# Twelve norm statistics of a decoder trunk from rounded high and low parts of the squares, a fourth relevance buffer, and selection steps placed later

## The reference

```python
def rms_norm(x, gain):
    xf = x.astype(jnp.float32)
    y = xf * lax.rsqrt(jnp.mean(xf * xf, axis=-1, keepdims=True) + RMS_EPS)
    return (y * gain.astype(jnp.float32)).astype(x.dtype)
...
    q_d = rms_norm(heads(d_q, DSA_HEADS), dsa_q_norm)
    k_d = rms_norm(heads(d_k, DSA_HEADS), dsa_k_norm)
...
    q_m = heads(rms_norm(m_cq, mla_q_latent_norm) @ mla_w_uq, MLA_HEADS)
    kv_m = heads(rms_norm(m_ckv, mla_kv_latent_norm) @ mla_w_ukv, MLA_HEADS)
    q_m = rms_norm(q_m, mla_q_norm)
    k_m = rms_norm(jnp.concatenate([k_nope, k_rope], axis=-1), mla_k_norm)
...
        rel = jax.nn.relu(jnp.einsum('bqhd,bsd->bqhs', iqb, ik))
        score = jnp.einsum('bqhs,bqh->bqs', rel, iwb).astype(jnp.float32)
        score = jnp.where(visible[None], score, NEG_INF)
        _, idx = lax.top_k(score, top_k)
```

## Time and profile before

| what | value |
|---|---|
| median of 3 runs | 1255.1 us (1255.06 to 1255.46) |
| the profiled execution | 1255.26 us, of which its span is 1253.5 us |
| PE busy | 1237.1 us, 99% of the span |
| DVE busy | 751.8 us, 60% |
| ACT busy | 528.8 us, 42% |
| POOL busy | 217.1 us, 17% |
| granted TensorE clock | 1.00 of full speed throughout |
| chain that ended last | PE 92%, ACT 3%, DVE 3%, issue 1%, DMA 1% |

### The profile page before, as it was taken

How to read it: one execution, slowest core, us unless ns; L and a number is a source line. 1 busy time by engine, 2 the same in 40 slices (tenths; PEclk the granted TensorE clock), 3 DMA queues, 4 the chain that set the end, 5 groups by cost and what they waited for, 6 DMA issues and landing times.

```text
span 1253.5 us, 17688 instructions
## 1 busy us (share of the span) xinstructions
PE 1237.1 (99%) x5956; PEld 973.9 (78%) x5956; DVE 751.8 (60%) x1233; ACT 528.8 (42%) x858; POOL 217.1 (17%) x141
## 2 busy tenths in 40 slices
PE   9999999999999999999999999999999999999998
PEld 7766876688888888888886668767888888888887
DVE  6689868644644554544756898685446445445444
ACT  5674438644223224224436643586432242232331
POOL 1122330020120110200621334200201102102002
PEclk9999999999999999999999999999999999999999
DMA  6212220033233223323222212201232223233223
GB/s 245 86 51 67 68 85 2 18 101 123 92 101 100 98 86 100 100 88 99 98 85 85 67 51 85 68 2 40 95 100 87 99 100 101 84 100 100 96 94 111
DMA packets 30720, 108.36 MB, mean 86 GB/s; under 512 B 3536, under 2 KB 3536, under 8 KB 30672
## 3 DMA queue, kind: packets, MB, share of 16 engines
q1 hardware_dynamic: 29520, 103.82, 24.9%
q0 software_dynamic: 432, 2.86, 0.6%
q10 hardware_dynamic: 720, 1.07, 0.3%
HBM read 105.64 MB, written 2.10 MB: 86 GB/s over the span
## 4 chain that ended last, share of the span: by engine, by line
PE 92%; ACT 3%; DVE 3%; issue 1%; DMA 1%; ACTq 0%; DVEq 0%
PE bank L889 19%; PE bank L890 19%; PE bank L891 19%; PE bank L510 6%; PE bank L512 6%; PE bank L511 6%; PE bank L533 2%; PE bank L532 2%; PE bank L531 2%; PE bank L546 2%; PE bank L772 2%; PE bank L784 1%; PE bank L799 1%; PE bank L750 1%; DMA x<-in_x 1%
## 5 line engine op out<-in xcount | busy, mean ns | idle before, releaser
L944 ACT ACTIVATE wh<-raw 128x1024 fp32r<-128x1024 f32 x191 | 201.6, 1055 | 382.7 <-PE bank L891 246.5
L1267 DVE TENSOR_TENSOR wl<-raw,wh 128x1024 fp32r<-128x1024 f32 x155 | 241.2, 1556 | 75.8 <-ACT wh L944 75.7
L889 PE MATMUL bank<-hh,wl 128*128 128x512 f32 x512 | 200.0, 391 | 0.0
L889 PE MATMUL bank<-xmh,wl 128*128 128x512 f32 x512 | 199.3, 389 | 0.0
L891 PE MATMUL bank<-hl,wh 128*128 128x512 f32 x512 | 199.2, 389 | 0.0
L890 PE MATMUL bank<-xmh,wh 128*128 128x512 f32 x512 | 199.2, 389 | 0.0
L891 PE MATMUL bank<-xml,wh 128*128 128x512 f32 x512 | 199.2, 389 | 0.0
L890 PE MATMUL bank<-hh,wh 128*128 128x512 f32 x512 | 199.2, 389 | 0.0
L476 POOL TENSOR_TENSOR x<-x,rsb 128x512 f32<-128x512 f32 x63 | 83.3, 1322 | 589.3 <-DVE rsb L1688 589.3
L510 PE MATMUL bank<-xgh,wl 128*128 128x512 f32 x368 | 151.3, 411 | 3.6 <-DVE xgl L1280 3.4
L1677 DVE TENSOR_TENSOR sqb<-tf 128x512 f32<-128x512 f32 x64 | 44.3, 692 | 181.6 <-ACT hh L1230 181.6
(11 more groups left out here) (215 smaller groups left out, 1641.5 us busy)
## 6 DMA issues: line engine op xcount, KB each, us to landing
raw<-in_stream SPq DMA_DIRECT2D x191, 512.0 KB, 3.3
out_y<-x SPq DMA_DIRECT2D x8, 256.0 KB, 3.6
x<-in_x ACTq DMA_DIRECT2D x4, 256.0 KB, 6.9
x<-in_x SPq DMA_DIRECT2D x4, 256.0 KB, 7.2
con<-in_consts POOLq DMA_DIRECT2D x1, 976.5 KB, 5.2
par<-in_params POOLq DMA_DIRECT2D x1, 916.0 KB, 5.0
par<-in_params POOLq DMA_DIRECT2D x1, 896.0 KB, 6.9
raw<-in_stream SPq DMA_DIRECT2D x2, 256.0 KB, 4.2
```

The source lines that it names most:

```text
L889: pe.matmul(B.t[s][:], wl[:, s, n_block(k)], src_h[:, k], start=(k == 0), stop=False)
L944: act.activation(wh[:, s], raw[:, s], ACT.Copy).then_inc(hi_ready.sem, 1)
L1267: vec.tensor_tensor(wl[:, s], raw[:, s], wh[:, s], ALU.subtract).then_inc(lo_ready.sem, 1)
```

## The change

Five things are changed.

1. For the twelve statistics, ACT squares into `sqb` and then copies `sqb` into a rounded `sqh` (fp32r); DVE writes `sql = sqb - sqh` (fp32r, `square_low`); PE does two fp32r passes, `sqh` and `sql`, with a rounded matrix of ones or blocks (`stat_parts`), where it did one float32 product. `sqh` and `sql` lie in memory that is free in this stage. `low_rows` and `turn_rows` products stay float32 and now come first.
2. The ring of relevance buffers has four places (`RELS`), the fourth in the memory of `gg`.
3. On ACT, the square of `ckv` stands ahead of `relevant(3)` and that of `dqst0` between the two factors of slot 8.
4. The selection steps: one fewer in slots 9, 10 and 14, one more in 19, 20 and 21.
5. At the end of layer 0 DVE adds the last block of `x` itself, with the low part of block 6 ahead of it and that of the last weights behind it; POOL's running sum of squares follows.

```diff
+RELS = 4
...
+                def square_high(name, src, rows=slice(0, P), wait=None):
+                    i = norm_index(name)
+                    if wait is not None:
+                        act.wait_ge(*wait)
+                    link(act.activation(sqb[rows, i % 2], src, ACT.Square))
+                    act.activation(sqh[rows, i % 2], sqb[rows, i % 2], ACT.Copy).then_inc(nsq_ready.sem, 1)
...
+                def square_low(name, rows=slice(0, P)):
+                    i = norm_index(name)
+                    vec.wait_ge(*nsq_ready.at(l, i))
+                    vec.tensor_tensor(sql[rows, i % 2], sqb[rows, i % 2], sqh[rows, i % 2], ALU.subtract)\
+                        .then_inc(nsl_ready.sem, 1)
...
+            def stat_parts(l, name, lhsT, rows=P):
+                i = norm_index(name)
+                pe.wait_ge(*nsl_ready.at(l, i))
+                pe.wait_ge(*B.vacant(l, name))
+                pe.matmul(B[name][0:rows, :], lhsT, sqh[0:rows, i % 2], start=True, stop=False)
+                return pe.matmul(B[name][0:rows, :], lhsT, sql[0:rows, i % 2], start=False, stop=True)
...
-                        if i >= 3:
-                            act.wait_ge(*rel_used.at(l, i - 3))
+                        if i >= RELS:
+                            act.wait_ge(*rel_used.at(l, i - RELS))
...
                     if u == 7:
+                        square_high("ckvst", ckvn[:], wait=B.freed(l, "ckv"))
                         relevant(3)
-                        square("ckvst", ckvn[:], wait=B.freed(l, "ckv"))
...
                         factor("cqst", Q_RANK)
+                        square_high("dqst0", dqr[:, 0], wait=B.freed(l, "dq0"))
                         factor("ckvst", KV_RANK)
-                        square("dqst0", dqr[:, 0], wait=B.freed(l, "dq0"))
                         relevant(5)
...
-                per_slot = {9: 4, 10: 4, 11: 3, 12: 3, 13: 3, 14: 3, 15: 3, 16: 4, 17: 4, 18: 4,
-                            19: 4, 20: 4, 21: 3, 22: 2}
+                per_slot = {9: 3, 10: 3, 11: 3, 12: 3, 13: 3, 14: 2, 15: 3, 16: 4, 17: 4, 18: 4,
+                            19: 5, 20: 5, 21: 4, 22: 2}
...
-                    for d in range(KB):
+                    for d in range(KB - 1):
                         share(GROUPS - 1, d // 2, d % 2)
                         if d >= 1:
                             gained_low(l + 1, 0, d - 1, xgh, xgl, G_ATTN)
+                    gained_low(l + 1, 0, KB - 2, xgh, xgl, G_ATTN)
+                    share(GROUPS - 1, 3, 1, lows=False)
+                    vec.wait_ge(*dn_freed[1].at(l, GROUPS * 4 - 1))
+                    vec.wait_ge(*x_ready.at(l + 1, -2))
+                    vec.tensor_tensor(x[:, KB - 1], x[:, KB - 1], rsb[:, 1], ALU.add).then_inc(x_ready.sem, 1)
+                    low_part(1, hi_ready.at(l + 1, 1))
                     gained_low(l + 1, 0, KB - 1, xgh, xgl, G_ATTN)
```

More of the change, by code:

```diff
@@ L202 @@
 VEC_LINKS = 400
-ACT_LINKS = 2
+N_PARTS = 12
+ACT_LINKS = 2 + N_PARTS
 def build_trunk(nc, x_in, stream, params, consts, out):
@@ L480, in _ @@
                         add_share(g, d)
-                for d in range(KB - final):
+                for d in range(KB - 1):
                     add_share(GROUPS - 1, d)
@@ L667, in _ @@
                 unit(8, before=midway(4))
-                pe.wait_ge(*nsq_ready.at(l, 0))
+                pe.wait_ge(*nsl_ready.at(l, 0))
                 pe.wait_ge(*B.vacant(l, "cqst"))
-                pe.wait_ge(*rows_ready.at(0, 4))
-                pe.matmul(B["cqst"][:], ones[:], sqb[:, 0], start=True, stop=False)
-                pe.matmul(B["cqst"][:], low_rows[:], lnb[:], start=False, stop=True)\
+                pe.wait_ge(*rows_ready.at(0, 5))
+                pe.wait_ge(*blk_ready.at(0, 0))
+                pe.matmul(B["cqst"][:], low_rows[:], lnb[:], start=True, stop=False)
+                pe.matmul(B["cqst"][:], ones_r[:], sqh[:, 0], start=False, stop=False)
+                pe.matmul(B["cqst"][:], ones_r[:], sql[:, 0], start=False, stop=True)\
                     .then_inc(*B.on_fill("cqst"))
-                stat(l, "ckvst", ones[:], sq_of("ckvst"))
+                stat_parts(l, "ckvst", ones_r[:]).then_inc(*B.on_fill("ckvst"))
                 relevance(5)
                 unit(9)
-                stat(l, "dqst0", blk, sq_of("dqst0"))
+                stat_parts(l, "dqst0", blk_r[:]).then_inc(*B.on_fill("dqst0"))
                 mla_q(0)
@@ L1095, in tasks @@
                         factor("dqst0", DH)
-                        square("dqst1", dqr[:, 1], wait=B.freed(l, "dq1"))
+                        square_high("dqst1", dqr[:, 1], wait=B.freed(l, "dq1"))
                     if u == 10:
@@ L1100, in tasks @@
                         factor("dqst1", DH)
-                        square("dkst0", dkn[:, 0], wait=B.freed(l, "dk0"))
+                        square_high("dkst0", dkn[:, 0], wait=B.freed(l, "dk0"))
                     if u == 11:
@@ L1105, in tasks @@
                         factor("dkst0", DH)
-                        square("dkst1", dkn[:, 1], wait=B.freed(l, "dk1"))
+                        square_high("dkst1", dkn[:, 1], wait=B.freed(l, "dk1"))
                     if u == 12:
@@ L1112, in tasks @@
                         factor("mqst3", QK, QK)
-                        square("mkst0", B["mk0"][:], wait=B.filled(l, "mk0"))
+                        square_high("mkst0", B["mk0"][:], wait=B.filled(l, "mk0"))
                     if u == 14:
-                        square("mkst1", B["mk1"][:], wait=B.filled(l, "mk1"))
+                        square_high("mkst1", B["mk1"][:], wait=B.filled(l, "mk1"))
                     if u in (14, 15):
@@ L1465, in tasks @@
                         weighted(2)
+                        square_low("cqst")
                     if u == 7:
+                        square_low("ckvst")
                         weighted(3)
@@ L1479, in tasks @@
                                                  ALU.mult, ALU.mult).then_inc(nrs_used.sem, 1)
+                        square_low("dqst0")
                         f = use_factor("ckvst")
@@ L1485, in tasks @@
                         mla_turn(0)
+                        square_low("mqst0", slice(0, QK))
                         dsa_queries(0)
+                        square_low("dqst1")
                     if u == 10:
@@ L1497, in tasks @@
                         mla_turn(3)
+                        square_low("mqst3", slice(0, QK))
                         dsa_keys(1)
@@ L1507, in tasks @@
                               *krb_ready.at(l, 0))
+                        square_low("mkst0")
                     if u in (14, 15):
```

50 lines of the change are left out of this document (35 added, 15 removed).

## The result

The changed kernel takes 1272.6 us (median of 4 runs, 1270.55 to 1276.97), the kernel before on the same chip 1255.1 (1255.06 to 1255.46). The ratio is 1.0138, 95% interval 1.0116 to 1.016: 17.5 us slower. Forecast were 1270.7 us, range 1262 to 1274. The profiled execution took 1270.55 us, its span 1268.7; it is the fastest of the four and 15.3 us above the profiled execution before. The other 2 us of the median lie in runs that left no profile.

A forecast was written before the change was run, and what follows sets the result against it. PE sets the end with DVE close behind; DVE becomes the bound in slots 9 to 13. Two layers lose 8.7 us each (+17.4), the boundary gains 1.8: 1270.7 us from 1255.1, range 1262 to 1274.

The forecast's parts named there:

- PE's saving and DVE's load: PE could save 9.6 us, but in slots 9 to 13 DVE's load becomes 43.9 us and bounds the stretch.
- rival C: Collisions stay away or cost little, DVE's load alone decides: 1252.7 to 1254.5 us; chance 0.12.
- Groups 4 and 5: In both relevance groups POOL asks 2.13 us behind ACT's gate or factor, beating a DVE addition; DVE loses 2.15 us each.
- Slot 9: After unit 10 POOL asks at 84.45 and delays DVE's subtraction for mqst0; unit 11 ends at 96.7, loss 4.0 us.
- rival B: One collision, in group 5 or slot 9, is missed; each layer loses 5 to 7 us, 1263 to 1267; chance 0.16.
- Slots 12 and 13: kinv and slot 13's last addition meet POOL (2.15 and 1.4 us); mkst0 lags 4.9 us; loss 8.9 at unit 15.
- The sum: 8.7 us lost per layer, +17.4 for two layers, less 1.8 at the boundary: 1270.7 us.
- The boundary: Between the layers, PE's late start of blocks 6 and 7 shrinks: gain 1.8 us, bounds 1.0 to 1.9.
- The ring: A fourth relevance buffer shrinks PE's 4.1 us of waits, but in group 4 POOL gets in and DVE loses 2.15 us.
- The rule on DVE and POOL: A DVE instruction with two SBUF inputs and a POOL one exclude each other by issue order: 2.07 us against 0.78.

The follow-up runs named there:

- e3: The changed kernel with four more selection steps moved out of slots 10 to 13 to slots 21 and 22; 1260.51 us.
- e8: The changed kernel with POOL's low parts of the blocks for units 8 to 17 cut to 512 of 1024 columns; 1263.12 us.
- f3: As f2, with the last five statistics (mqst2, dkst1, mqst3, mkst0, mkst1) in two passes; 1246.24 us.
- e4: The changed kernel with 20 more rounded passes of PE in front of the wait for mkst0's squares; 1271.99 us.
- e1: The kernel before with part 5 of the change (the boundary) alone; 1253.21 us.
- f4: The kernel before with the changed kernel's boundary and the steps of f2, three relevance buffers, float32 statistics; 1253.18 us.
- e7: The kernel before with a fourth relevance buffer and nothing else; 1263.65 us.
- f2: The kernel before with a fourth relevance buffer, the changed kernel's boundary and seven fewer selection steps in slots 9 to 14, float32 statistics; 1248.03 us.
- e2: The changed kernel with three relevance buffers instead of four; 1269.02 us.
- e5: The changed kernel with three relevance buffers and four more selection steps moved out of slots 10 to 13; 1251.34 us.

## Why the prediction was right, step by step

**PE's saving and DVE's load.** DVE was taken as the bound of slots 9 to 13 and was: slot 10 took it 8.59 us (86.54 to 95.13, forecast 8.7), units 12 and 13 came 8.6 us apart at the same pace (8.1 in e3), and PE waited for ten subtractions, 4.9 us in all. The subtraction was taken at 0.72 us from start to start; it took 0.61 in most places (84.56 to 85.17), 0.71 in others (85.83 to 86.54). That DVE's load alone (rival C) does not make the loss is shown from the other side: with POOL's part halved half the loss goes (e8), with the load lowered by four steps slots 12 and 13 lose nothing (e3), and with DVE 98% busy but in time there is a gain (f3). Neither alone: the load makes DVE late, being late brings it into POOL's parts, and these make it later still.

**Groups 4 and 5.** Both collisions came, at 2.11 us behind the gate and behind the factor where 2.13 stood, with 2.5 to 3.0 us for what took 0.5 to 1.0. The 0.25 us by which the one in group 5 hung was 0.15.

**Slot 9: the step that failed.** "POOL asks 1.15 later at 84.45, ... unit 11 ends at 96.7, now 92.7. Loss 4.0." In the profiled execution POOL started at 85.86, the subtraction took 0.69 us and unit 11 lost 1.8. The stall of about 2 us in front of it was in the forecast (of 1.8 us won only 0.4 were left), but not that the clock would be at 0.50 behind it: unit 10 ended at 84.73 instead of 83.3, and POOL's request with it. By this the collision that rival B leaves out was left out in this slot, with another cause than the one given, and without rival B's price of 5 to 7 us per layer. Where the clock held, in e3 and in layer 0 of e4, the step came as written: 84.30 and 84.00 for POOL, 2.48 and 2.47 us for the subtraction, 4.11 us of waiting, and on top a slow clock that the forecast did not have (unit 11 at 97.87 and 97.93).

**Slots 12 and 13.** `kinv` (2.85 us) and the `krot` addition (2.17), 4.88 us before `mkst0`: all as written. The size was off: from unit 14 to unit 15 the loss grew by 7.0 us (table above, 1.8 to 8.8), where the forecast had 4.5 (4.4 to 8.9). The 2.5 us between them are the slow clock, and e4 shows them (2.2 and 2.6).

**The sum.** 8.4 us in layer 0 and 8.9 in layer 1, against 8.7 forecast. That it fits so closely is luck, since two errors cancel: in layer 0 2.6 us too much up to unit 14, 2.3 too little from there to unit 18. Both come from the one thing left out, that PE went on at half speed behind its stalls. A forecast with the clock behind `mkst0`, but with the collision in slot 9 kept, would have said about 11 us per layer (8.7 + 2.4), some 1275 us in all and above the range.

**The boundary.** Forecast 1.8, measured 2.1 to 2.4 (e1, f4), above the bound of 1.9. The term was mis-sized: the earlier trace rows give 1.01 us for block 6 and 1.01 for block 7, 2.0 in all, and I had 1.9 and then took off 0.1; what the last 0.1 to 0.4 are is open. No row of PE waits there now; block 6 and 7 of the changed kernel follow without a gap:

```profile
641.12 0.39 PE L524 MATMUL bank<-xgh,wl 128*128 128x512 f32 x1
...
641.80 0.39 PE L524 MATMUL bank<-xgh,wl 128*128 128x512 f32 x1
```

**The ring.** The prediction put it down as a gain of PE's waits that the collision of group 4 spoils. Alone it costs 8.2 us (e7), with lighter slots it gives 5.2 (f2). That it would cost so much alone, and that it would be paid at `mv0`, seven units behind group 4, stood in no step.

**The rule on DVE and POOL.** At 84.30 in e3 POOL got in while DVE read PSUM (until 84.68), and the subtraction with two SBUF operands that came 0.41 us behind it waited for all of POOL's instruction. The Trainium skill, SBUF — State Buffer, section Who interferes with whom, says that such a pair locks each other out for a whole instruction, by the order in which they ask. By that rule the trace agrees, also in e8, where `kinv` is held up for 1.07 us instead of 2.17 by half an instruction of POOL.

## What to carry to other kernels

Before work is given to a second engine in a full stretch, ask when the first one will want it, and what the second engine's neighbours do at that moment: here the same twelve subtractions in each layer cost 15.8 us or brought 1.9 (e2 and e5, both layers together), by where four selection steps stood. A wait removed makes a later part of the program run earlier against everything that did not move, so follow its consumers until DVE or whoever else is late has caught up; the bill for the fourth buffer came seven units later. And count with the slow clock in the price of a stall of PE: here it followed all stalls of 3.2 us and more, and some 2 us beyond the wait is what one cost.
